# Seven products instead of eight for six chunks of every group's up projection, in a two-layer trunk kernel

## The reference

```python
for l in range(DEPTH):                      # 2
    h = rmsnorm(x, norm_mix[l])
    o_a, o_b = dsa_branch(...), swa_branch(...)   # 8 sparse heads, 16 sliding-window heads, T5 bias each
    merged = g_a * (o_a @ w_branch_a[l]) + g_b * (o_b @ w_branch_b[l])
    x = x + merged @ w_out[l]
    h = rmsnorm(x, norm_mlp[l])
    x = x + jnp.square(jax.nn.relu(h @ w_up[l])) @ w_down[l]      # 2048 -> 8192 -> 2048
return rmsnorm(x, final_norm)
```

## Time and profile before

| what | value |
| --- | --- |
| median of 3 runs | 2712.03 us (2709.22 to 2713.03) |
| the profiled execution itself | 2718.1 us |
| its span, first to last instruction | 2716.4 us |
| busy: PE, DVE, ACT | 2696.5, 1768.3, 1365.0 us |
| granted clock of PE, mean share of the full one | 0.998 |
| DMA, mean | 212 GB/s |

### The profile page before, as it was taken

How to read it: one execution, slowest core, us unless ns; L and a number is a source line. 1 busy time by engine, 2 the same in 40 slices (tenths; PEclk the granted TensorE clock), 3 DMA queues, 4 the chain that set the end, 5 groups by cost and what they waited for, 6 DMA issues and landing times.

```text
span 2716.4 us, 35283 instructions
## 1 busy us (share of the span) xinstructions
PE 2696.5 (99%) x12756; PEld 2212.7 (81%) x12756; DVE 1768.3 (65%) x2538; ACT 1365.0 (50%) x1735; POOL 21.0 (1%) x29
## 2 busy tenths in 40 slices
PE   9999999999999999999999999999999999999998
PEld 7788778888888887888887887788888888888886
DVE  5565555556686785876656655555666957769665
ACT  5445554445554555545445455544455545455443
POOL 0000000000000000000000000000000000000000
PEclk9999999999999999999999999999999999999999
DMA  7875545676766666667666655566776666676664
GB/s 240 249 229 164 185 155 186 219 230 232 235 215 210 228 199 229 205 218 238 225 219 217 212 171 179 160 202 219 229 251 230 199 223 222 203 231 210 216 226 154
DMA packets 189697, 574.76 MB, mean 212 GB/s; under 512 B 21432, under 2 KB 56856, under 8 KB 189408
## 3 DMA queue, kind: packets, MB, share of 16 engines
q1 hardware_dynamic: 188000, 568.67, 64.0%
q0 software_dynamic: 1152, 3.80, 0.7%
...
## 4 chain that ended last, share of the span: by engine, by line
PE 94%; DMA 2%; DVE 1%; issue 1%; ACT 0%; SPq 0%; ACTq 0%; POOLq 0%; POOL 0%; DVEq 0%
PE acc L444 28%; PE acc L445 28%; PE acc L446 28%; DMA scratch<-spread 1%; PE acc L412 1%; PE acc L413 1%; PE acc L414 1%; PE att L412 1%; PE att L414 1%; PE att L413 1%; DMA moved<-scratch 1%; PE turn L413 0%; PE turn L414 0%; PE turn L412 0%; PE att L502 0%
## 5 line engine op out<-in xcount | busy, mean ns | idle before, releaser
L1095 DVE TENSOR_TENSOR w_lo<-raw,w_hi 128x1024 fp32r<-128x1024 f32 (+1 forms) x866 | 1040.9, 1213 | 598.0 <-ACT w_hi L742 596.3
L742 ACT ACTIVATE w_hi<-raw 128x1024 fp32r<-128x1024 f32 (+1 forms) x866 | 903.3, 1051 | 747.3 <-PE acc L446 688.4
L444 PE MATMUL acc<-w_hi,h_hl 128*128 128x512 f32 x2176 | 866.9, 398 | 2.6 <-DVE w_lo L1095 2.1
L446 PE MATMUL acc<-w_hi,h_hl 128*128 128x512 f32 x2176 | 859.3, 395 | 0.0
L445 PE MATMUL acc<-w_lo,h_hl 128*128 128x512 f32 x2176 | 859.1, 395 | 0.0
L444 PEld LDWEIGHTS acc<-w_hi,h_hl 128*128 128x128 f32 x2176 | 409.9, 188 | 105.2 <-DVE w_lo L1095 5.7
L446 PEld LDWEIGHTS acc<-w_hi,h_hl 128*128 128x128 f32 x2176 | 409.8, 188 | 96.9
L445 PEld LDWEIGHTS acc<-w_lo,h_hl 128*128 128x128 f32 x2176 | 410.1, 188 | 94.1
L444 PE MATMUL acc<-w_hi,o_hl 128*128 128x512 f32 x1064 | 421.5, 396 | 0.3 <-DVE o_hl L1193 0.2
L445 PE MATMUL acc<-w_lo,o_hl 128*128 128x512 f32 x1064 | 420.0, 395 | 0.0
L446 PE MATMUL acc<-w_hi,o_hl 128*128 128x512 f32 x1064 | 419.8, 395 | 0.0
...
## 6 DMA issues: line engine op xcount, KB each, us to landing
...
bias_b<-bias_rows POOLq DMA_DIRECT2D x4, 384.0 KB, 8.2
...
```

The lines of the kernel that those rows point to most:

```text
L444: nc.tensor.matmul(o, a_hi, hi[:, kk], start=(k == 0), stop=False)
L446: last = nc.tensor.matmul(o, a_lo, hi[:, kk], start=False, stop=fin)
L742: nc.scalar.activation(w_hi[s][:, 0:2 * width], raw[r][:, 0:2 * width], ACT.Copy).then_inc(hi_ready, 1)
L1095: nc.vector.tensor_tensor(w_lo[s][:, 0:2 * width], raw[r][:, 0:2 * width], w_hi[s][:, 0:2 * width].bitcast(F32), ALU.subtract).then_inc(lo ...
```

## The change

It does four things. (1) Chunks 1, 3 and 5 of up0 and up2, in all four groups, are multiplied by seven products (`WIDE_UP`). PE's side banks for up0 are `wide_acc[0]`, for up2 `wide_acc[1]`. (2) The output of such a unit has to be put together before the relu: ACT copies a quarter of the side bank to `stage` (`take_side`, at chunk 3 of the next unit), DVE makes five operations of it (`add_up_sides`, at chunk 3), ACT's relu then reads `stage` and moves, with the square, to chunk 4, as do DVE's transposes (`finish`). (3) The inputs h need their sums, once per layer: six DVE operations and a hi and lo copy in each of output units 1 to 3, kept in `s_hh`. (4) `s_hh` shares its memory with `bias_b`. So bias_b is loaded again in layer 0 once up2 of the last group is done; the rows are written in 8 copies instead of 32, in one transfer, and read in 16 pieces of 8 partitions, waited for in pairs, `bias_a` first. Signs of two input sums are turned, which takes their negations away.

```diff
-COPIES = 32
+COPIES = 8
+WIDE_UP = ((1, 3, 5), (), (1, 3, 5), ())
@@ gpsimd
             for i in range(BIAS_PIECES):
...
+                if i % 2:
+                    pool.wait_ge(bias_a_loaded, 16 * (i + 1))
...
+                if i < 2 * DEPTH and i % 2 == 0:
+                    pool.wait_ge(multiplied, (i // 2 - 1) * CHUNKS + C_MLP + 64 * (GROUPS - 1) + 24 + SLOTS)
+                    load_bias_b(i // 2)
@@ tensor, up
-                         hold=[(0, moved_took, took_of(E_XO + 2)), (6, moved_took, took_of(E_XO + 3))]
-                         if n == 0 and isinstance(g, int) else ())
+                         hold=[(0, moved_took, took_of(E_XO + 2)), (1, h_sums_took, H_SUMS * (l + 1)),
+                               (6, moved_took, took_of(E_XO + 3))] if n == 0 and isinstance(g, int) else (),
+                         wide=WIDE_UP[n], sum_of=h_sum, sides=wide_acc[n // 2])
@@ scalar
+                def take_side(g, n):
+                    unit_done(l * CHUNKS + g * 64 + (C_MLP + 8 * (n + 1)))
+                    act.wait_ge(spread_ready, g * NBLK + (l * MOVES + E_U + n))
+                    nc.scalar.activation(stage[:, 0, HALF:NB], wide_acc[n // 2][0][:, HALF:NB], ACT.Copy).then_inc(sides_out, 1)
                 def take_up(g, n):
+                    if WIDE_UP[n]:
+                        act.wait_ge(up_summed, g * 2 + (l * (2 * GROUPS) + n // 2 + 1))
...
+                        src = stage[:, t, :] if WIDE_UP[n] else acc[n % 2][t][:]
+                        last = nc.scalar.activation(stage[:, t, :], src, ACT.Relu, scale=rms[:, 0, t:t + 1])
@@ vector
+                    nc.vector.tensor_scalar(a22, x22, g1, None, ALU.mult)
+                    chain.link(nc.vector.tensor_scalar(a11, x11, g0, None, ALU.mult))
+                    nc.vector.scalar_tensor_tensor(out=s3, in0=x21, scalar=g0, in1=a11, op0=ALU.mult, op1=ALU.subtract)
+                    chain.link(nc.vector.scalar_tensor_tensor(out=s1, in0=x21, scalar=g0, in1=a22, op0=ALU.mult, op1=ALU.add))
+                    chain.link(nc.vector.tensor_tensor(s2, s1, a11, ALU.subtract))
+                    nc.vector.scalar_tensor_tensor(out=s4, in0=x12, scalar=g1, in1=s2, op0=ALU.mult, op1=ALU.subtract)\
+                        .then_inc(h_summed, 1)
...
+                def add_up_sides(g, n):
...
+                    dve.wait_ge(sides_out, at + 1)
+                    nc.vector.tensor_tensor(side_sum, z[:, 0:HALF], quarters[:, 1, :], ALU.add).then_inc(up_step, 1)
+                    dve.wait_ge(up_step, steps + 1)
+                    nc.vector.tensor_tensor(quarters[:, 0::3, :], side_sum.unsqueeze(1).to_broadcast([P, 2, HALF]),
+                                            w[:].rearrange("p (h c) -> p h c", h=2), ALU.subtract).then_inc(up_step, 1)
+                    dve.wait_ge(up_step, steps + 2)
+                    nc.vector.tensor_tensor(quarters[:, 2, :], quarters[:, 3, :], w[:, 0:HALF], ALU.subtract).then_inc(up_step, 1)
+                    nc.vector.tensor_tensor(stage[:, 0, :], acc[n % 2][0][:], stage[:, 0, :], ALU.add)
+                    dve.wait_ge(up_step, steps + 3)
+                    nc.vector.tensor_tensor(stage[:, 1, :], acc[n % 2][1][:], stage[:, 1, :], ALU.add).then_inc(up_summed, 1)
...
+                        if WIDE_UP[n - 1]:
+                            take, finish = (lambda: add_up_sides(g, n - 1)), take
```

More of the change, by code:

```diff
@@ L141, in trunk_kernel @@
         bias_a = sb("bias_a", [P, A_HEADS, SEQ])
-        bias_b = sb("bias_b", [P, B_HEADS, WINDOW_KEYS])
+        with nc.sbuf_tensor("bias_b", [P, B_HEADS, WINDOW_KEYS], F32) as bias_b:
+            pass
+        s_hh = sb("s_hh", [P, 2, H_SUMS, 4 * P], F32R)
         stage = sb("stage", [P, TT, NB])
@@ L394, in turn_into, with seven_products, sums @@
                 last.then_inc(turned, 1)
[L396 removed]
+            def seven_products(c, banks, lhs, sum_of, sides, chunks):
                 hi, lo = w_hi[c % SLOTS], w_lo[c % SLOTS]
[L399 to L401 removed]
+                first, final = c == chunks[0], c == chunks[-1]
                 def block(t, kk):
[L404 to L407 removed]
+                    return [lhs(part, 2 * c + kk, t) for part in range(2)]
+                def sums(i):
+                    return [sum_of(part, c // 2, i) for part in range(2)]
                 def product(a, b, o, start, stop):
@@ L432, in unit @@
                     pe.wait_ge(lo_ready, cl + (RAW + c + 1))
-                    if wide is not None and c in WIDE[wide]:
-                        seven_products(c, banks, wide).then_inc(multiplied, 1)
+                    if c in wide:
+                        seven_products(c, banks, lhs, sum_of, sides, wide).then_inc(multiplied, 1)
                         continue
@@ L442, in unit @@
                             o = banks[t][:, 0:width]
-                            fin = k == 2 * chunks - 1 or (wide is not None and 7 in WIDE[wide] and k == 13)
+                            fin = k == 2 * chunks - 1 or (7 in wide and k == 13)
                             nc.tensor.matmul(o, a_hi, hi[:, kk], start=(k == 0), stop=False)
@@ L758, in unit @@
                         take()
+                    if c == 4 and finish:
+                        finish()
                     if c in wide:
```

152 lines of the change are left out of this document (93 added, 59 removed).

## The result

| | before | after |
| --- | --- | --- |
| median | 2711.06 us (4 runs) | 2754.25 us (4 runs, 2750.56 to 2761.49) |
| the profiled execution | 2718.1 us | 2761.49 us |
| PE, DVE, ACT busy | 2696.5, 1768.3, 1365.0 us | 2700.2, 1924.3, 1404.1 us |

The ratio after to before is 1.0162, interval 1.0138 to 1.0187: 43 us slower. The prediction said 10 us slower and at most 2736. The profiled execution is the slowest of the four, 7.2 us above their median, so what its trace shows as lost is more than the typical execution loses.

A forecast was written before the change was run, and what follows sets the result against it. The prediction took PE's stream of matmuls to bound the kernel. Stalls of 6.6 + 9.7 + 2.4 + 5.2 = 23.9 us less a gain of 13.9 made +10.0 us, so 2722 us, range 2701 to 2736.

The forecast's parts named there:

- A: Passages up1 to up2 and up3 to down0: chunk 7 just in time, chunk 0 late; 0.55 x 12, 6.6 us.
- D: First up unit: PE waits at chunk 3 for w_lo, 2.6 us in each of 2 layers, 5.2 us.
- Gain, 13.9: PE, up0 and up2: 48 seven-product chunks, each 0.29 us shorter than a plain one, save 13.9 us.
- Rival 4: PE: a 256-column pair costs 0.75 of a 512-column one, +42 us, 2754 us; chance 0.01.
- The shift of the relu, 3.3: After up0 and up2: rebuilding the output makes the relu start 3.3 us later, 2.7 to 4.0.
- B: down0 and down1: o_hl's last quarter comes late at chunk 6, the rest waits in down1; 1.62 x 6, 9.7 us.
- C: up2, chunk 7: ready at U + 19.0 (U: unit's first matmul), wanted at 18.6; 0.4 x 6, 2.4 us.
- The last group ... no stall there.: Last group: computes no input sums, which gives 0.9 + 0.6 us back, so no stall.
- Rival 3: Lateness breeds lateness: raw slots freed late, all landings take 9.9 us; 18 us more, 2740 us; chance 0.07.
- Costed at nothing: Bias loads on POOL, more but smaller: bias_b at most 66 us, covered by 111 us, so no cost.

The follow-up runs named there:

- e4: The changed kernel with SP's fetch of the turned piece ahead of the load of chunk 7 instead of behind it; 2739.43 us, ratio 1.0114.
- e12: The changed kernel with all chunks of the up units plain, but the longer way of up0 and up2 to the relu kept; 2733.37 us, ratio 1.0083.
- e2: The changed kernel without the second load of bias_b in layer 0's last group; 2752.45 us, ratio 1.0155.
- e3: The changed kernel with PE's loop over three turns written out, the other engines keeping theirs; 2748.37 us, ratio 1.0127.
- e1: The kernel before with the changed kernel's bias loading alone, without the second load; 2708.93 us, ratio 0.9991.
- e6: The changed kernel with only chunk 5 of each layer's first up unit by seven products, instead of 1, 3 and 5; 2728.70 us, ratio 1.0069.
- e17: e10 with only chunk 3 of down0 by seven products instead of 1 and 3; 2704.54 us, ratio 0.9978.
- e10: The changed kernel with chunk 5 alone in the first up unit, the fetch ahead of chunk 7's load and PE's loop written out; 2728.44 us, ratio 1.0058.

## Why the prediction was wrong in size

The direction, the mechanism (a longer way to the relu, landing in units without lead) and the places A to D were right. The sum of the waits was not: 23.9 us predicted, 64.0 lost in the trace. By its own steps, lost in PE beyond the 5.7 us of before:

- **Gain, 13.9.** Right: 2.51 us per chunk, and the account closes with 0.29 N. Rival 4, the page's rule, is out on the starts; that its 2754 is the time that came is chance.
- **The shift of the relu, 3.3.** Right: 3.25.
- **D, 5.2 predicted, 16.2 lost.** The step that failed most. Chunk 3 was priced well in layer 0 (2.5, a wait of 2.7; 3.0 lost) and too low in layer 1 (4.5 lost). "2.5 us, with 0.1 for chunk 4" left out the hold at chunk 6, where 8.4 of the 16.2 were lost. The last quarter of h starts its way 4.2 us later in DVE's order, and I had counted DVE and ACT behind adding to x, but not SP, whose fetch stands behind a load that waits for that same late w_lo. In e4's trace 11.4 of the 16.2 are gone.
- **B, 9.7 predicted, 15.0 lost (17.8 less 2.8).** The transposes' place was right: U of down0 is 751.13, they end at 756.97, 5.84 later against 5.9 predicted. The landing was mis-sized: 8.7 taken, 9.9 measured (756.97 to 766.89), and 8.8 to 10.1, 9.4 on average, over the six groups. I had read it from one group; over six it was 9.0 in the kernel before already. Its store is what varies, and what the store stands behind in SP's queue goes with it:

```profile
728.03 1.47 SPq L283 DMA_DIRECT2D raw<-in_w_main  x2
735.72 0.33 SPq L294 DMA_DIRECT2D scratch<-spread  x1
...
738.63 1.75 SPq L300 DMA_DIRECT2D moved<-scratch  x4
740.63 15.63 SPq L283 DMA_DIRECT2D raw<-in_w_main  x7
756.99 0.33 SPq L294 DMA_DIRECT2D scratch<-spread  x1
...
760.79 1.75 SPq L300 DMA_DIRECT2D moved<-scratch  x4
```

```profile
755.67 1.30 DVE L1217 STREAM_TRANSPOSE spread<-stage 128x512 f32<-128x512 f32 x2
...
766.89 1.06 ACT L835 ACTIVATE o_hl<-moved 128x1024 fp32r<-128x1024 f32 x1 [6.29 <-DMA moved<-scratch]
```

In up3 the store (735.72) is issued 6.6 us behind a chunk's load and the fetch starts 2.9 us later. In down0 it is issued 1.1 us behind the last of seven loads, and the fetch starts 3.8 us later. In the MLPs of this trace the 12 stores issued under 1.5 us behind a load landed in 3.5 to 5.4 us, the 16 issued over 5 us behind one in 2.8 to 3.0.

- **C, 2.4 predicted, 4.8 lost.** The same landing: 8.9 to 10.2 in the four places that lost, 8.2 to 8.3 in the other two, whose transposes weren't late either.
- **A, 6.6 predicted, 11.3 lost.** Not the landing, which in up3 was 7.9 us on average before and 8.0 here. Chunk 0 was priced well (0.35 predicted, 0.37 lost per passage). Chunk 7, "just in time", lost 6.8 over the 12 passages: up3's transposes came 3.4 us later, which used up the lead of 3.4 that I had read in one place.
- **"The last group ... no stall there."** Wrong: 8.8 lost against 1.0. The longer way alone makes 5.0 (e12), without any seven-product chunk. The second load of bias_b may add to it: I had costed it only as POOL time and not for what its transfers do to the fetches beside them, and two fetches took 8 us there. How much is its own stays open, as said at e2.
- **The turn, not in the sum: 8.5.** PE's own jump (e3). The time that e3 gave back was 6 us, with intervals that just overlap.
- **The clock, not in the sum.** Its six falls, 10.2 us, stand in the losses above: 3.4 in D, 3.4 at the turn, 1.7 in B, 1.7 in the last group. The prediction priced each stop at its own length, as if the clock stayed at its upper level behind it, and gave no reason.
- **Costed at nothing: bias loading at the start.** Right in time (e1).

The sum of the additions is 64.0, less 13.9 is +50; measured between the two profiled executions 43.4, since that of before lay 6.5 high. By the medians, 2711.1 and 2754.3, it is 43 as well: there the typical execution of the changed kernel lies 7 us under the traced one, and by the same reckoning it loses some 57 us more than before. **Rival 3**, lateness breeds lateness, came nearest; I gave it 0.07 and 18 us, and its landings did come (B and C), but D, the turn, the last group and the clock were not in it. I had priced each wait from the leads of the kernel before, as if the one ahead of it left them alone. e6 (14 us of own loss, 25.5 of time) and e17 (24 us where 12 were expected from the waits) show that they don't add up so.

**Open.** Why the jumps lose 9.6 us here, 4.8 and 6.8 in e2 and e4, whose PE code is the same, and 1.1 in before; when the clock falls after a stop and when not; and why a store issued right behind a chunk's load lands anywhere from 3.5 to 5.5 us. That it shares the queues with that load is my guess: the times go with it, but no run moved the store alone. e17's stores, most of them just as close behind a load, landed 1 us sooner than e10's, which the guess doesn't explain.
